# Unused bytes between the tiles of a two-block kernel, so that all that TensorE reads begins at one remainder of 512 bytes

## What is computed

```python
def first_block(x, ...):
    for l in range(DEPTH):
        x = hybrid_layer(x, attn_norm_w[l], w_in[l], ..., peer_down[l], peer_up[l])
    return x

def second_block(x, mem, ...):
    for l in range(DEPTH):
        h = rmsnorm(x, norm_mix[l])
        p = h @ w_in[l]
        ...
        merged = g_a * y_a + g_b * y_b + g_c * y_c
        x = x + merged @ w_o[l]
        h = rmsnorm(x, norm_xa[l])
        mm = rmsnorm(mem, norm_mem[l])
        x = x + cross_attention(h, mm, xa_q[l], xa_k[l], xa_v[l], xa_o[l])
        h = rmsnorm(x, norm_ffn[l])
        x = x + (jax.nn.silu(h @ w1[l]) * (h @ w3[l])) @ w2[l]
    return rmsnorm(x, final_norm)
```

## The kernel before

| tiles | remainder of 512 before |
|---|---|
| `h_t`, `h_t_lo`, `ring`, `ring_lo`, `x_res`, `common_sb` | 128 |
| `h_t_expert` | 192 |
| `out_hi`, `out_lo`, `coef_hi`, `coef_lo`, `held_hi`, `held_lo`, `up_hi`, `up_lo`, `down_hi`, `down_lo`, `first_hi`, `gate_hi`, `lead_x_hi`, `lead_x_lo`, `h_t_hi`, `ya_hi`, `branch_lo`, the arena | 32 |
| `w_hi`, `mt_hi`, `mt_lo`, `ff_hi`, `ff_lo` | 224 |
| `branch_hi` | 288 |

## Time and profile before

### The profile page before, as it was taken

The page is one execution under the profiler, slowest core; times in us unless marked ns, Lnnn a source line. Parts: engine busy times, 40 slices in busy tenths (PEclk is TensorE's granted clock), DMA queues, the critical chain, the costliest instruction groups (busy, mean ns, idle before and its releaser), DMA issues.

```text
span 2832.9 us, 45798 instructions
## 1 busy us (share of the span) xinstructions
PE 2808.2 (99%) x18566; PEld 2530.0 (89%) x18566; DVE 1946.6 (69%) x2882; ACT 1426.8 (50%) x1771; POOL 148.3 (5%) x145
## 2 busy tenths in 40 slices
PE   8999999999999999999999999999999999999998
PEld 7899998899999889999888999988899988888997
DVE  7889989555555788998955555576756556565664
ACT  6654554544444675355454444455455445545543
POOL 0033110000000002311000000000000000000000
PEclk9999999999999999999999999999999999999999
DMA  6443666855554534466686455465555656554663
GB/s 213 123 163 137 216 233 203 292 218 189 196 190 151 183 116 157 149 210 231 198 294 228 178 194 191 163 214 171 180 169 178 187 191 181 170 184 151 178 187 133
DMA packets 219570, 530.21 MB, mean 187 GB/s; under 512 B 13546, under 2 KB 87440, under 8 KB 208400
## 3 DMA queue, kind: packets, MB, share of 16 engines
q1 hardware_dynamic: 212944, 504.32, 53.6%
q0 software_dynamic: 6464, 23.61, 2.3%
HBM read 507.81 MB, written 20.06 MB: 186 GB/s over the span
## 4 chain that ended last, share of the span: by engine, by line
PE 97%; DVE 2%; DMA 1%; issue 0%; ACT 0%; SPq 0%; DVEq 0%; ACTq 0%
PE ps L2666 17%; PE ps L2648 13%; PE ps L1539 13%; PE ps L1549 12%; PE ps L1527 12%; PE ps L1482 11%; PE ps L608 4%; PE ps L599 4%; PE ps L1453 2%; PE ps L2925 2%; PE ps L1464 1%; PE ps L1254 1%; PE ps L2834 0%; PE ps L2818 0%; DMA ring<-in_peer_down 0%
## 5 line engine op out<-in xcount | busy, mean ns | idle before, releaser
L2267 DVE TENSOR_TENSOR ring_lo<-ring,w_hi 128x1024 fp32r<-128x1024 f32 x320 | 388.4, 1224 | 242.6 <-ACT w_hi L2263 241.3
L2263 ACT ACTIVATE w_hi<-ring 128x1024 fp32r<-128x1024 f32 x320 | 335.2, 1056 | 235.3 <-PE ps L2666 168.7
L1539 PE MATMUL ps<-h_t_lo,down_hi 128*128 128x256 f32 x1024 | 288.2, 281 | 0.0
L1539 PE MATMUL ps<-h_t_expert,down_lo 128*128 128x256 f32 x1024 | 287.8, 281 | 0.0
L1539 PE MATMUL ps<-h_t_expert,down_hi 128*128 128x256 f32 x1024 | 286.8, 280 | 0.0
L2648 PE MATMUL ps<-h_t_lo,w_hi 128*128 128x256 f32 x928 | 260.8, 281 | 0.0
L2648 PE MATMUL ps<-h_t_hi,w_hi 128*128 128x256 f32 x928 | 259.4, 280 | 0.1
L2648 PE MATMUL ps<-h_t_hi,ring_lo 128*128 128x256 f32 x928 | 259.0, 279 | 0.0
L1142 ACT ACTIVATE out_hi<-ring 128x1024 fp32r<-128x1024 f32 x128 | 135.7, 1060 | 162.4 <-PE ps L1527 155.8
L2034 DVE TENSOR_TENSOR up_lo<-ring,up_hi 128x2048 fp32r<-128x2048 f32 x64 | 146.7, 2292 | 99.7 <-ACT up_hi L1133 99.7
L2027 DVE TENSOR_TENSOR out_lo<-ring,out_hi 128x1024 fp32r<-128x1024 f32 x128 | 156.5, 1223 | 77.7 <-ACT out_hi L1142 77.7
(11 more groups left out here) (532 smaller groups left out, 7447.2 us busy)
## 6 DMA issues: line engine op xcount, KB each, us to landing
ring<-in_peer_down SPq DMA_DIRECT2D x128, 1024.0 KB, 5.1
ring<-in_w_in SPq DMA_DIRECT2D x140, 512.0 KB, 3.7
ring<-in_peer_up SPq DMA_DIRECT2D x66, 1024.0 KB, 4.8
ring<-in_w SPq DMA_DIRECT2D x132, 512.0 KB, 3.7
ring<-in_peer_up SPq DMA_DIRECT2D x124, 512.0 KB, 4.4
late_gates<-arena POOLq DMA_DIRECT2D x64, 256.0 KB, 2.7
arena<-late_gates SPq DMA_DIRECT2D x16, 1024.0 KB, 6.3
ring<-in_w_out SPq DMA_DIRECT2D x16, 512.0 KB, 3.9
```

The source lines that it names most:

```text
L1539: m = pe.e.matmul(PS[:, 4 + b, j * T:(j + 1) * T], w[:, b, o], x[:, kc, :], start=kc == 0 and n == 0, stop=kc == KD - 1 and n == 2)
L2263: a.e.activation(W_HI[:, g % HI_SLOTS, :], RAW[:, g % RAW_SLOTS, :], ACT.Copy).then_inc(*a.count(f"c{g}_hi"))
L2267: v.e.tensor_tensor(RAW_LO[:, g % RAW_SLOTS, :], RAW[:, g % RAW_SLOTS, :], W_HI[:, g % HI_SLOTS, :].bitcast(F32), ALU.subtract).then_inc(* ...
```

## The change

Two unused tiles are declared (448 bytes behind `common_sb`, 160 bytes behind `stat`), and three sizes of unused or padded room are rounded to 512 bytes instead of 64. Every tile behind them moves by 448 to 1376 bytes. As built, all tiles of the table above then begin at remainder 128; those that were there stay where they are. The instructions, 20212 in the program, are the same in the same order on every engine, with the same semaphores; only addresses differ.

```diff
-N_SPAR = -(-N_SECOND // 16) * 16
-N_Z3 = -(-2 * (T + 2) // 16) * 16
+N_SPAR = -(-N_SECOND // 128) * 128
+N_Z3 = -(-2 * (T + 2) // 128) * 128
...
         COMMON = sb("common_sb", [P, N_COMMON])
+        sb("behind_common", [P, 112])
...
         STAT = sb("stat", [P, 128])
+        sb("behind_stat", [P, 40])
...
-            over("before_branch", [P, 4112], F32)
+            over("before_branch", [P, N_Z3 + 2 * T + TT * 1536], F32)
             BRANCH_HI = over("branch_hi", [P, 6, T])
```

## The result

| | before, same chip | after |
|---|---|---|
| median of 8 runs | 2835.12 us (2833.96 to 2838.34) | 2843.03 us (2841.20 to 2844.96) |
| the profiled execution's own time | 2834.7 us | 2842.92 us |
| its span | 2832.9 us | 2841.1 us |

The changed kernel is slower: 1.0025 times the time before, 95% interval 1.0015 to 1.0035. That is some 8 us, where 12 us less were forecast. In the changed kernel a line number is two higher than before (L1527 is L1529, L2648 is L2650, L2666 is L2668).

What follows compares the result with a forecast made beforehand. TensorE's matmul steps were taken to bound the kernel. From 2834.4 us, 11.9 us saved on wide matmuls and 0 for narrow matmuls and the other engines gave 2822 us, range 2802 to 2848.

Steps and rivals of the forecast that it cites:

- The bound: Whole kernel: TensorE's matmuls cover 99% of the span, so only time off a matmul's step comes off the total.
- ScalarE, VectorE, DMA at 0: Copies, subtractions and transfers: the moved addresses cost or save nothing there, 0 us.
- The wide term: 512-column matmuls going from mixed to equal remainders (2736) drop to L1527's 226.7 ns, 11.9 us saved.
- The far end of 215.9 ns (float32): 512-column matmuls: limit from below, all 5808 at the plain float32 row's step, 74 us saved.
- The narrow term: 256-column matmuls, 10176 of them: step expected unchanged on average, 0 us.
- the bound from above: 256-column matmuls: L1527's extra of 13.4 ns on 106.7 gives 120.0 ns, 18 us lost.
- the first rival: Narrow matmuls settle at 120.0 ns while wide ones gain as forecast: 2840 us, chance 0.23.
- The two ports: TensorE operand reads: by the skill's independent-ports rule remainders could not matter, saving 0 instead of 11.9 us; float32r rows disagree.
- The fineness: SBUF reads: by the skill's 16-byte-line rule no remainder beats another, sum 0; the spread of L2666 rows speaks against it.
- 128 isn't 32: Rival: the remainder itself counts, equal ones at 128 settle on the high step, 19 us lost, 2853 us; chance 0.13.
- nothing moves: Rival: something other than remainders makes L1527 and L2666 differ, so 2834 us; chance 0.16.
- both widths gain: Rival: narrow matmuls lose the 5.6 ns too, 57 us more saved, 2766 us; chance 0.10.

Runs made afterwards that it cites:

- The streams: Kernels computing nothing of the reference, only TensorE matmul streams at varied operand start addresses, other engines idle; equal remainders took 120.0 ns (256 columns) and 226.7 ns (512).
- the last kernel: Kernel before with unused bytes at ten places, setting the narrow streams' tiles apart; 2795.17 us against 2837.72, ratio 0.9854.
- the maps: Two TensorE-only kernels, 512 arrangements of operand starts by 32 bytes at each width, plus 4-byte offsets; 113.3 to 124.4 ns at 256 columns, 226.7 to 236.7 at 512.

## Why the prediction was wrong

- *The bound.* Right: a nanosecond off the step came off the time. With one pair of tiles moved L1541 took 18.7 us less, and the profiled execution 20.7 (2842.92 to 2822.26): 18.7 in L1541, 3.0 for the two falls of the clock and 0.7 for the start of the program, less the 1.6 of one late load.
- *ScalarE, VectorE, DMA at 0.* Right: 1223 and 1056 ns, as before, and no new wait in the chain.
- *The wide term.* Right in sign and mechanism. 264 matmuls on `ff` in 59.87 us, 59.8 said; L1529 174.11, unchanged. Of the sum of 11.9 us 10.0 came (and 0.4 in L1551, which was put at 0): `h_t`, sized as going from 231.0 to 226.7, went from 230.7 to 227.2 in the mean of its steps under 300 ns, which is 4.7 us instead of 5.8; the other three came 0.1 to 0.4 us short each. The far end of 215.9 ns (float32) was nowhere approached.
- *The narrow term, taken as 0.* This step failed, and with it the sign. It was +14.8 us, 1.5 ns a matmul, where the bound from above said 18: 129.60 us for 1080 is what the first rival had. Its mechanism was right. That its time, 2840, is only 3 us under the measured median is in part luck: its 18 and its 11.9 both came out smaller (14.8 and 10.4), which leaves 4.4 us where it had 6, and the profiled execution's clock added 3.7 that it did not have.

  I took 0 because the rows with two passes of three at equal remainders lie on both sides of the mixed ones. The streams show why that was no argument: the step does not approach 120.0 by degrees as more tiles agree. `mt`'s arrangement (224, 224, 224, 128), one tile away from equal, gives 117.8 alone, and equality of all four 120.0; other arrangements one tile away gave 117.0 to 120.0. A row that is near in how many tiles agree is not near in the step. The nearest row was the wide one with all equal, L1527, whose extra (13.4 ns) was the extra at 256 columns (120.0 - 106.7 = 13.3), so the bound worked out from it was the steady value. That the extra is the same at both widths held for equal remainders; it is no rule: 8 bytes apart it is 8.8 ns at 256 columns (115.5) and 17.4 at 512 (230.7).
- *The two ports.* The Trainium skill, TensorE: Matmul & The Clock Gate, section "Step-by-step: what each phase is for", says that loading the next weights takes no read bandwidth from the running matmul. That rule gives no reason for what the streams show: with all other engines idle, the same 256 columns take 113.3 to 124.4 ns by the start addresses of the operands alone. They do not refute it either, for no stream leaves the weight loads out, and whether the loads or the matmuls are held up stays open.
- *The fineness.* The Trainium skill, SBUF — State Buffer, section "Door 1: The DMA port swizzle", has reads at full bandwidth within a line of 16 bytes and a penalty at each new line. Offsets of 16 and 32 bytes, whole lines, give 118.3 ns and no offset gives 120.0, so tiles that all begin a line are not alike. The section does not reach this effect.
- *The other rivals.* "128 isn't 32" falls (all 16 remainders alike); "nothing moves" falls (idle engines, same steps); "both widths gain" is what this change did not do, though the last kernel shows that narrow ones can gain 4.4 ns.
- *Not in the prediction at all:* the clock, whose falls are 3.1 us and whose later rise at the start is 0.6 us of the profiled execution's 8.2.

## What to carry to other kernels

Where TensorE bounds and weight loads run under the matmuls, the step of float32r matmuls depends on how the start addresses of the moving and stationary tiles lie to each other, by 256 bytes; time it for each width in several streams of its own before placing tiles, since 256 columns were best with the tiles apart (113.3 ns) and 512 with them equal (226.7), and some arrangements give one step in one stream and another in the next. Don't settle an unmeasured arrangement from one that shares most of it. A case with all conditions met, even at another width, is worth a bound, and the bound belongs in the forecast as a term of weight; it is not a value until it is measured. A placing of the tiles costs no instruction, and was worth 1.5% of this kernel.

## What the runs showed of the hardware

- Equal remainders of all operands give one steady step whatever the remainder (120.0 and 226.7 ns), and the period is 256 bytes, but for two pairs of narrow streams and one of wide ones, of 24 each; nothing that was run at 512 columns is faster, much at 256 is.
- Over the 512 arrangements of the maps the spread by addresses alone is 10% at 256 columns (113.3 to 124.4 ns) and 4% at 512 (226.7 to 236.7); one offset outside them reached 243.3 at 512.
- Some arrangements have two or three steady steps, of which a stream settles on one and keeps it (113.3 or 117.8 at 64 bytes; 113.3, 117.8 or 120.0 at 52; at 512 columns 226.7 or 243.3 at 156). Why the addresses act so, and what would predict a step without measuring it, stays open.
- The granted clock fell to 1.2 GHz for some 3 us at one place of the first block in some executions, with TensorE shown busy in the rows ahead of it. What brings it on, and whether the changed kernel has it more often than the others, stays open.
